# A two-layer decoder trunk: the projection tiles of the double memory step are spread differently over its units

## The chip, the cores and the metric

One core of a Trainium2 chip. The metric is the device time of one execution, in microseconds (us). The engines: TensorE (PE) multiplies matrices, ScalarE (ACT) and VectorE (DVE) do everything elementwise, GpSimd (POOL) helps with copies and sums, SyncE's queue (SP) issues the weight loads. Every engine works through its own program in order; engines wait for each other through semaphores.

## The reference

A trunk of two layers on x of 512 x 1024, with 256 memory tokens, 12 mixing heads and 4 memory heads of 64 columns. Layer A mixes by chunked spatial gating, layer B by forgetting attention (FoX) with keys, values and forget gates from `kv_w`. In each layer the 4 memory heads attend to the memory:

```python
z = x @ b_w_q[j]                      # queries: 12 mixing heads, then 4 memory heads
kvf = x @ kv_w                        # keys, values, forget logits
logcum = cumsum(log_sigmoid(f_logit + kv_b_f))
mix = fox_attention(q, k_sh, v_sh, logcum)
p = softmax(qm . mk * scale);  mo = p . mv          # memory attention
y = concatenate([mix, mo]) @ w_o[layer]
x = layer_norm(DN_ALPHA * x + y);  x = layer_norm(DN_ALPHA * x + sq_relu_mlp(x))
```

## The kernel before

Activations are held transposed, as 8 tiles of 128 features x 512 tokens. Every float32 operand is split in a high and a low part (`x_hi`, `x_lo`, `w_hi`, `w_lo`), and a product is three matmuls: high by high, high by low, low by high. A projection block is 128 output columns: 8 k tiles (one for each 128 rows of the weight), so 24 matmuls of 512 columns into one PSUM bank. Its weight of 128 x 1024 is loaded by SP's queue into one of two places of `w_raw`; ScalarE writes the high part (`prepare`, L1066), VectorE the low one (`prepare`, L1464, which records at L1462) and raises `w_split`. The first k tile of a block waits for that semaphore; a block's last one raises `w_used`.

Layer B's attention is made in steps. A step works on 8 units; a unit is a block of 128 queries. For each unit, in order: PE makes scores (into one of two PSUM banks), VectorE takes the row maximum (`row_max`, L1518 in this step), ScalarE the exponentials (L1125), VectorE normalises them (L1528, L1532), PE transposes the result two units later (`turn`, L561), and ScalarE and VectorE write the high and the low part of the transposes. Behind the units PE does the attention products of each half of the step (`attend`).

The first such step of layer B is the double memory step (`STEP_B`): all 4 memory heads at once, two in each unit, and units 0 to 3 for the first pair of heads, 4 to 7 for the second. `attend_pair` makes each pair's products; that of pair 0 comes behind unit 7, that of pair 1 at the end of the step. Between, `cumulate` sums the forget gates over the tokens. The transposes' parts of pair 0 are called `pm_hi`, `pm_lo`, those of pair 1 `pn_hi`, `pn_lo`.

While PE would wait for the others it is given other work: a step carries the three projection blocks (queries, keys, values; 24 k tiles) that the next step needs. The list `at` in `pair_step` of PE's program says where: place n (`filler(n)`) makes the k tiles at[n] to at[n+1]. Tiles 0 to 7 are the query block, 8 to 15 the key block, 16 to 23 the value block. The order of PE's program within unit u is `filler(u)`, the transposes of unit u-2, the scores of unit u. Behind unit 7 come attention 0, transposes 6, `filler(8)`, transposes 7, `cumulate`, `filler(9)`, attention 1, and the transposes of the values (`turn_values`).

The other engines' programs have fixed places for what belongs to these blocks. ScalarE makes the key block's high part in unit 0, the value block's in unit 4, the next step's first in unit 7. VectorE makes the low parts in units 0 and 4, each directly behind that unit's row maximum, and the next step's first behind the transposes of unit 7; `qs` (queries) is written in units 2 and 3, the first half of the keys in `kc` in unit 6, the second after the units. The order of VectorE's program within a unit is row maximum, that low part, the low part of the transposes of unit u-2, normalising of unit u, `qs` or `kc`.

Behind attention 1 ScalarE and VectorE write its result (`mix_hi`, `mix_lo`), the values and the cumulated gates (`cum`), and two rows of `kc` from these; the scores of the next step wait for them. Five more such steps with keys, one without new blocks, the output projection, the layer norm and the MLP follow.

Of the kernel before, what the change touches and what calls it, by code (L numbers as in the profile page):

```python
# [63 lines left out]
def trunk_kernel(nc, x, mem, a_w_in, a_sgu_ln_g, a_sgu_ln_b, a_w_s, a_b_s, kv_w, kv_b_f, b_w_q,  # L64
# [41 lines left out]
    STEP_A, STEP_B, STEP_FOX, STEP_LAST = 0, 2, 3, 8  # L106
# [12 lines left out]
    with ctx:  # L119
# [261 lines left out]
        def double(s):  # L381

            return s.trip is None and s.base == STEP_B
# [5 lines left out]
        def ahead(s):  # L389

            return s.trip is None and s.base == STEP_LAST
# [117 lines left out]
        def _(pe):  # L509
# [12 lines left out]
            def project(b, g, hi, lo, columns=T, order=range(KT), ready=None, parts=(0, KT),  # L522
                        start=True, stop=True):

                bank = proj[g.slot]
                for n in range(*parts):
                    k = order[n]
                    if n == 0:
                        pe.wait_ge(w_split, b.at(1))
                        if start:  # L530
                            wait(pe, proj_free[g.slot], g.half())
                    if ready:
                        ready(n)
                    last = products(bank[:, 0:columns], block_terms(b, k, hi[:, k], lo[:, k]),
                                    start and n == 0, stop and n == KT - 1)
                if parts[1] == KT:
                    last.then_inc(w_used, 1)
# [85 lines left out]
            def turn(s, u):  # L623

                pe.wait_ge(probs_ready, s.at(u + 1, 8))
                tiles = [probs[:, u % 2, j * P:(j + 1) * P] for j in range(keys(s, u))]
                transposes(tr_index(s, u), tiles[::-1] if fox(s) and u >= TT else tiles)
# [16 lines left out]
            def attend(s, head):  # L644

                if double(s):
                    attend_pair(s, head)
                    return
                pe.wait_ge(tr_free, tr_index(s, head * TT + TT - 1).at(1))
                wait(pe, mix_ready, s.at(head - 1, 2))  # L650
                c = step_kind(s).slot
                if fox(s) and head == 0:
                    pe.wait_ge(vt_ready, step_kind(s).at(1))
                tiles = TT if fox(s) else MT
                for j in range(tiles):
                    seen = slice(j * P if fox(s) else 0, T)
                    if fox(s):
                        vh, vl = v_hi[:, c, j], v_lo[:, c, j]
                    else:
                        vh, vl = mv_hi[:, j, c * P:(c + 1) * P], mv_lo[:, j, c * P:(c + 1) * P]  # L660
                    ph, pl = seen_places(s, head, j)
                    last = products(pv[head][:, seen], [(vh, ph), (vh, pl), (vl, ph)], j == 0, j == tiles - 1)
                last.then_inc(pv_done, 1)

            def turn_values(s, j):

                g = j.times(3, G_FOX + 2)
                pe.wait_ge(proj_free[g.slot], g.half(2))
                if double(s):
                    pe.wait_ge(exp_done, s.at(8, 8))  # L670
                else:
                    pe.wait_ge(mix_ready, s.at(1, 2))
                for t in range(TT):
                    last = pe.transpose(values_bank(s)[:, t * P:(t + 1) * P], v_tmp[:, g.slot, t * P:(t + 1) * P], ident[:, :])
                last.then_inc(vt_done, 1)

            def pair_step(s, b=None, g=None, values=None, extra=None):

                at = [0, 5, 7] if s.base in (STEP_A, STEP_B) else [0, 3, 6]
                at += [8, 11, 14, 16, 18, 19, 21, 24]

                def filler(n):
                    if b is not None:
                        c = at[n] // KT
                        project(b.plus(c), g.plus(c), x_hi, x_lo, parts=(at[n] - c * KT, at[n + 1] - c * KT))
                    elif extra:
                        for part in extra.get(n, ()):  # L690
                            out_start(1, *part)
                for u in range(8):
                    filler(u)
                    if ahead(s):
                        scores(s, u)
                    if u >= 2:
                        turn(s, u - 2)
                    if not ahead(s):
                        scores(s, u)
                attend(s, 0)  # L700
                turn(s, 6)
                filler(8)
                turn(s, 7)
                if s.base == STEP_B:
                    cumulate()
                filler(9)
                attend(s, 1)
                if values is not None:
                    turn_values(s, values)
# [45 lines left out]
            def out_start(layer, c, n):  # L755

                def ready(n):
                    if layer:
                        pe.wait_ge(mix_ready, 2 * STEP_B + n + 1 if n < 2 else 2 * (STEP_FOX + n - 2) + 2)
                    elif n < 2:  # L760
                        pe.wait_ge(mix_ready, 2 * n + 2)
                    else:
                        pe.wait_ge(sgu_ready, 2 * (n - 1))
                project(Pos(B_WO[layer] + c), Pos(G_WO[layer] + c), mix_hi, mix_lo, order=out_order,
                        ready=ready, parts=(n, n + 1))
# [207 lines left out]
            def cumulate():  # L973

                pe.wait_ge(f_act, 3)
                pe.wait_ge(f_step, 5)
                pe.wait_ge(tri_set, 2)
                pe.wait_ge(exp_done, 8 * STEP_B + 7)
                for t in range(TT):
                    span = tri_r[:, 0:T - t * P]  # L980
                    last = products(sc[0][:, t * P:T], [(lf_hi[:, t], span), (lf_lo[:, t], span)],
                                    t == 0, t == TT - 1)
                last.then_inc(cum_done, 1)
# [31 lines left out]
            for s in range(2):  # L1015
                pair_step(Pos(STEP_A + s), Pos(B_AU + 3 * s), Pos(G_AU + 3 * s))
# [23 lines left out]
            turn_forget_gate()  # L1040
            pe.wait_ge(lf_ones, 2)
            pair_step(Pos(STEP_B), Pos(B_FOX), Pos(G_FOX), values=Pos(0))
            with pe.Fori(0, 2) as i:
                for j in range(2):
                    pair_step(Pos(STEP_FOX + j, i, 2), Pos(B_FOX + 3 * (j + 1), i, 6),
                              Pos(G_FOX + 3 * (j + 1), i, 6), values=Pos(j + 1, i, 2))
# [1084 lines left out]
```

## Time and profile before

| | us |
|---|---|
| median of 3 runs | 1207.45 |
| lowest, highest | 1206.73, 1207.56 |
| the profiled execution | 1207.21 |
| its span, first to last instruction | 1205.5 |
| PE, DVE, ACT, POOL busy | 1161.2, 632.7, 491.2, 129.3 |
| mean granted clock of PE | 0.992 |

The profile is one execution. The double step's first projection tile starts 598.31 us after the span's start. Times of instructions are from there too. A matmul's start is a record, its end is modelled; where matmuls follow each other the distance between starts says what one costs. PE's granted clock is 1.00 at 2.4 GHz and 0.50 at 1.2 GHz.

### The profile page before, as it was taken

The page shows a single profiled execution, that of the slowest core. Times are in us where ns is not written, and L with a number is a line of the kernel's source. Part 1 is how long each engine was busy: PE and PEld are TensorE (multiplying, and loading weights), DVE is VectorE, ACT ScalarE, POOL GpSimd, SP SyncE. Part 2 cuts the span into 40 slices and gives each one's busy share as a digit, 9 for nine tenths or more (in the row PEclk, how much of TensorE's full clock was granted, in tenths as well). Part 3 has the DMA queues.
Part 4 walks back from the last instruction along what each step waited for, and adds up shares of the span by engine and source line. Part 5 has one row for each costly group of instructions (what it writes and reads, how often), then busy time and mean ns, then how long its engine had stood idle before and what let it go on. Part 6 is the DMA issues. An engine that isn't in the chain of part 4 may idle for free.

```text
span 1205.5 us, 16763 instructions
## 1 busy us (share of the span) xinstructions
PE 1161.2 (96%) x5888; PEld 976.6 (81%) x5888; DVE 632.7 (52%) x1032; ACT 491.2 (41%) x852; POOL 129.3 (11%) x156
## 2 busy tenths in 40 slices
PE   5998999999999999999998999999999999999997
PEld 5777779888888888789877888878888888888886
DVE  4477766644332445345576777866544323445226
ACT  4445535634211333224665555635543212334120
POOL 2300025100000000023300000026200000000000
PEclk9999999999999999999998999999999999999999
DMA  7422122333323333332311122212333333333332
GB/s 219 134 70 71 53 90 86 88 89 103 105 87 104 88 101 91 105 88 73 86 35 53 54 70 62 60 53 84 93 104 90 102 104 87 88 98 93 105 105 87
DMA packets 185590, 107.22 MB, mean 89 GB/s; under 512 B 4482, under 2 KB 180162, under 8 KB 185540
## 3 DMA queue, kind: packets, MB, share of 16 engines
q1 hardware_dynamic: 180112, 99.36, 28.5%
q10 hardware_dynamic: 5428, 7.18, 1.9%
q8 instruction: 32, 0.52, 0.2%
q14 instruction: 18, 0.15, 0.0%
HBM read 104.43 MB, written 2.10 MB: 88 GB/s over the span
## 4 chain that ended last, share of the span: by engine, by line
PE 74%; DVE 4%; ACT 4%; issue 3%; POOL 1%; DMA 0%; DVEq 0%; ACTq 0%; POOLq 0%; SPq 0%
PE proj L513 59%; PE pv L513 3%; PE sc L513 2%; PE proj L846 2%; PE pv L846 2%; PE tr L846 2%; PE sc L846 2%; PE tr L561 1%; DVE w_lo L1462 1%; ACT w_hi L1066 1%; ACT x L1232 1%; ACT x_hi L1234 1%; POOL total L2054 0%; DVE split_lo L1462 0%; POOL total L2064 0%
## 5 line engine op out<-in xcount | busy, mean ns | idle before, releaser
L1462 DVE TENSOR_TENSOR w_lo<-w_raw,w_hi 128x1024 fp32r<-128x1024 f32 x173 | 219.6, 1270 | 172.3 <-ACT w_hi L1066 124.2
L513 PE MATMUL proj<-x_hi,w_hi 128*128 128x512 f32 (+1 forms) x768 | 300.5, 393 | 1.9 <-ACT relu L1097 1.0
L513 PE MATMUL proj<-x_hi,w_lo 128*128 128x512 f32 (+1 forms) x768 | 295.9, 386 | 0.0
L513 PE MATMUL proj<-x_lo,w_hi 128*128 128x512 f32 (+1 forms) x768 | 289.8, 384 | 0.0
L1066 ACT CAST w_hi<-w_raw 128x1024 fp32r<-128x1024 f32 x160 | 166.9, 1044 | 168.6 <-PE proj L513 166.9
L513 PEld LDWEIGHTS proj<-x_hi,w_hi 128*128 128x128 f32 x768 | 146.1, 190 | 28.9 <-ACT x_hi L1234 2.2
L513 PEld LDWEIGHTS proj<-x_hi,w_lo 128*128 128x128 f32 x768 | 145.8, 190 | 29.2
L513 PEld LDWEIGHTS proj<-x_lo,w_hi 128*128 128x128 f32 x768 | 143.1, 189 | 25.7
L513 PE MATMUL proj<-h_hi,w_hi 128*128 128x512 f32 (+1 forms) x384 | 146.4, 381 | 2.5 <-DVE w_lo L1462 2.5
L513 PE MATMUL proj<-h_lo,w_hi 128*128 128x512 f32 (+1 forms) x384 | 146.0, 380 | 0.0
L513 PE MATMUL proj<-h_hi,w_lo 128*128 128x512 f32 (+1 forms) x384 | 146.0, 380 | 0.0
L1755 DVE TENSOR_TENSOR h_raw<-relu 128x512 f32<-128x512 f32 x64 | 44.3, 692 | 157.7 <-ACT relu L1097 157.7
L1097 ACT ACTIVATE relu<-proj 128x512 f32<-128x512 f32 x64 | 38.2, 597 | 196.0 <-PE proj L513 196.0
L513 PEld LDWEIGHTS proj<-h_hi,w_hi 128*128 128x128 f32 x384 | 72.2, 188 | 16.8 <-DVE w_lo L1462 3.1
L513 PEld LDWEIGHTS proj<-h_lo,w_hi 128*128 128x128 f32 x384 | 72.2, 188 | 13.8
L513 PEld LDWEIGHTS proj<-h_hi,w_lo 128*128 128x128 f32 x384 | 72.2, 188 | 13.7
L1129 ACT ACTIVATE probs<-sc,neg_max 128x128 f32<-128x128 f32 (+2 forms) x64 | 33.0, 516 | 55.9 <-DVE neg_max L1521 54.9
L2005 POOL TENSOR_TENSOR x_lo<-x,x_hi 128x256 fp32r<-128x256 f32 (+1 forms) x56 | 48.5, 875 | 58.0 <-ACT x L1230 24.8
L1462 DVE TENSOR_TENSOR h_lo<-h_raw,h_hi 128x512 f32 (+1 forms) x64 | 44.3, 692 | 14.9 <-ACT h_hi L1246 14.4
L2054 POOL TENSOR_TENSOR total<-x 128x512 f32<-128x512 f32 x3 | 4.5, 1499 | 440.9 <-DVE x L1672 440.9
L513 PE MATMUL proj<-mix_hi,w_hi 128*128 128x256 f32 (+1 forms) x128 | 45.8, 358 | 2.5 <-DVE w_lo L1462 2.2
L1665 DVE SCALAR_TENSOR_TENSOR x<-x,proj 128x512 f32 (+1 forms) x22 | 15.1, 687 | 61.0 <-PE proj L513 61.0
(344 smaller groups left out, 1805.4 us busy)
## 6 DMA issues: line engine op xcount, KB each, us to landing
w_raw<-in_w_up SPq DMA_DIRECT2D x64, 512.0 KB, 4.0
w_raw<-in_w_down SPq DMA_DIRECT2D x64, 512.0 KB, 3.6
w_raw<-in_w_o SPq DMA_DIRECT2D x16, 512.0 KB, 3.6
w_raw<-in_a_w_in SPq DMA_DIRECT2D x14, 512.0 KB, 3.8
w_raw<-in_kv_w SPq DMA_DIRECT2D x12, 512.0 KB, 3.9
w_raw<-in_mem_w_kv SPq DMA_DIRECT2D x8, 512.0 KB, 4.9
w_raw<-in_b_w_q SPq DMA_DIRECT2D x8, 512.0 KB, 3.6
x_nat<-in_x ACTq DMA_DIRECT2D x2, 1024.0 KB, 11.4
```

The costliest lines, as they stand in the source:

```text
L513: last = pe.matmul(target, lhs, rhs, start=start and n == 0, stop=stop and n == len(terms) - 1)
L561: last = pe.transpose(tr[t.slot][0:n, at:at + rows], piece, ident[0:rows, 0:rows])
L846: last = pe.matmul(rows_of[t][n][:, :], lhs, rhs, start=False, stop=stop and m == 2, skip_group_check=True)
L1066: act.copy(weights(b)[0], w_raw[:, b.slot]).then_inc(w_hi_ready, 1)
L1097: act.activation(target, proj[g.slot][:, 0:target.shape[-1]], function).then_inc(proj_free[g.slot], 1)
L1129: act.activation(probs[:, u % 2, 0:n], sc[u % 2][:, 0:n], ACT.Exp, bias=neg_max[:, u:u + 1], accum_out=row_sum[:, u:u + 1]).then_inc(exp_d ...
L1232: act.activation(x32[:, k, own], x32[:, k, own], ACT.Identity, **gain).then_inc(fin_ready, 1)
L1234: act.copy(x_hi[:, k, own], x32[:, k, own]).then_inc(x_hi_ready, 1)
L1462: return dve.tensor_tensor(target, whole, hi.bitcast(F32), ALU.subtract)
L1665: dve.scalar_tensor_tensor(out=tile if target is None else target, in0=tile, scalar=ALPHA if first else 1.0, in1=proj[g.slot][:, :], op0=A ...
L1755: dve.tensor_tensor(raw, wide, wide, ALU.mult).then_inc(relu_sq, 1)
L2005: pool.tensor_tensor(x_lo[:, k, own], x32[:, k, own], x_hi[:, k, own].bitcast(F32), ALU.subtract).then_inc(x_ready, 1)
```

## The change

The list of places for the double step gets its own numbers; the other steps keep theirs (the step in question took the list of `STEP_A` before).

```diff
--- before.py
+++ after.py
@@ -679,8 +679,10 @@
 
 
 
-                at = [0, 5, 7] if s.base in (STEP_A, STEP_B) else [0, 3, 6]
+                at = [0, 5, 7] if s.base == STEP_A else [0, 3, 6]
                 at += [8, 11, 14, 16, 18, 19, 21, 24]
+                if double(s):
+                    at = [0, 6, 8, 11, 13, 16, 18, 20, 21, 22, 24]
 
                 def filler(n):
                     if b is not None:
```

As k tiles of each place, for the double step: 5, 2, 1, 3, 3, 2, 2, 1, 2, 3 before and 6, 2, 3, 2, 3, 2, 2, 1, 1, 2 after. The key block (tile 8) starts at place 2 and not 3, the value block (tile 16) at place 5 and not 6. The programs of the other engines are as before.

## Rows read from the trace of the kernel before

**Rows 1.** The page's busy times: us (share of the span), instructions of each engine.

```profile
PE 1161.2 (96%) x5888; PEld 976.6 (81%) x5888; DVE 632.7 (52%) x1032; ACT 491.2 (41%) x852; POOL 129.3 (11%) x156
```

**Rows 2.** Stretches (us from start): length, busy us (instructions) by engine, granted clock, DMA.

```profile
core 0: us, PE busy (x) PEld busy (x) DVE busy (x) ACT busy (x) POOL busy (x), PEclk, DMA share, GB/s
598.30:634.25 35.95, 33.25 (x170) 27.16 (x169) 25.53 (x58) 24.39 (x60) 2.65 (x4) 0.95 0.13 36
634.25:640.45 6.20, 2.69 (x14) 1.97 (x13) 4.42 (x7) 3.18 (x5) 0.00 (x0) 0.90 0.23 70
661.60:688.00 26.40, 26.40 (x145) 22.49 (x144) 20.36 (x44) 15.23 (x36) 2.44 (x4) 1.00 0.22 61
```

**Rows 3.** PE in order of time: start, us, engine, line, operation, [idle before <- releaser].

```profile
598.31 0.50 PE L513 MATMUL proj<-x_hi,w_hi 128*128 128x512 f32 x1
...
601.86 0.28 PE L513 MATMUL sc<-mk_rest,qm 128*128 128x256 f32 x1
...
602.33 0.40 PE L513 MATMUL proj<-x_hi,w_hi 128*128 128x512 f32 x1
...
607.04 0.66 PE L561 MATMUL tr<-ident,probs 128*128 128x128 f32 x4 [1.98 <-DVE probs L1532]
...
609.27 0.63 PE L513 MATMUL proj<-x_lo,w_hi 128*128 128x512 f32 x1
609.70 0.63 PE L513 MATMUL proj<-x_hi,w_lo 128*128 128x512 f32 x1
...
612.45 0.28 PE L513 MATMUL sc<-mk_twice,qm 128*128 128x256 f32 x1
...
617.72 0.28 PE L513 MATMUL sc<-mk_twice,qm 128*128 128x256 f32 x1
618.13 0.50 PE L513 MATMUL proj<-x_hi,w_hi 128*128 128x512 f32 x1
...
619.61 0.60 PE L561 MATMUL tr<-ident,probs 128*128 128x128 f32 x4
...
620.40 0.28 PE L513 MATMUL sc<-mk_twice,qm 128*128 128x256 f32 x1
620.52 0.40 PE L513 MATMUL proj<-x_hi,w_hi 128*128 128x512 f32 x1
...
629.41 0.45 PE L513 MATMUL proj<-x_hi,w_hi 128*128 128x512 f32 x1
...
631.53 0.39 PE L513 MATMUL pv<-pn_hi,mv_hi 128*128 128x512 f32 x1
...
640.45 0.44 PE L513 MATMUL sc<-kc,qc 128*128 128x128 f32 x1 [3.51 <-DVE kc L1614]
```

**Rows 4.** VectorE in order of time, same columns.

```profile
604.07 1.22 DVE L1462 TENSOR_TENSOR w_lo<-w_raw,w_hi 128x1024 fp32r<-128x1024 f32 x1
...
609.40 0.69 DVE L1518 TENSOR_REDUCE neg_max<-sc 128x2 f32<-128x512 f32 x1
...
612.02 0.68 DVE L1596 SCALAR_TENSOR_TENSOR qs<-proj,qs 64x512 fp32r<-64x512 f32 x1
612.77 0.69 DVE L1518 TENSOR_REDUCE neg_max<-sc 128x2 f32<-128x512 f32 x1
...
616.13 0.69 DVE L1518 TENSOR_REDUCE neg_max<-sc 128x2 f32<-128x512 f32 x1
616.85 1.23 DVE L1462 TENSOR_TENSOR w_lo<-w_raw,w_hi 128x1024 fp32r<-128x1024 f32 x1
...
619.32 0.68 DVE L1518 TENSOR_REDUCE neg_max<-sc 128x2 f32<-128x512 f32 x1
...
621.82 0.68 DVE L1518 TENSOR_REDUCE neg_max<-sc 128x2 f32<-128x512 f32 x1
...
630.50 0.69 DVE L1462 TENSOR_TENSOR pn_lo<-tr,pn_hi 128x512 fp32r<-128x512 f32 x1
```

**Rows 5.** Stretches again, at the lower granted clock.

```profile
608.60:611.90 3.30, 3.30 (x11) 2.52 (x10) 2.67 (x8) 2.27 (x8) 0.15 (x1) 0.50 0.01 2
640.50:646.00 5.50, 5.50 (x16) 4.63 (x17) 1.83 (x5) 0.46 (x2) 0.00 (x0) 0.50 0.33 95
```

## The prediction

> **What bounds the kernel now.** First the page's busy times: TensorE works for 1161.2 of 1205.5 us, VectorE for 632.7, ScalarE for 491.2 [rows 1]. So time is saved or lost where PE stands still or runs at its lower clock. The busy time by stretch shows where that is: a key/query step further on is PE from end to end (26.40 of 26.40 us, granted clock 1.00), while the double step is not (33.25 of 35.95 us at 0.95), and in the 6.20 us behind it PE works 2.69 [rows 2]. The instructions in order of time give the places: the first transposes wait 1.98 us for `probs`, and the next step's first scores 3.51 for `kc` [rows 3]; unit 5's transposes show a short wait of the first kind.
>
> The question is whether the waits for `probs` are PE's to lose. They are not. VectorE goes round: row maximum of unit u, (ScalarE's exponentials), reciprocal, normalising, row maximum of unit u+1. The maxima of units 2 to 6 start at 609.40, 612.77, 616.13, 619.32 and 621.82 [rows 4]. The scores for them lay ready: the last score matmul of unit 5 was issued at 617.72 and ended at 618.00, 1.3 us ahead of its maximum [rows 3, 4]. Only unit 3 is near PE: its last one ends at 612.45 + 0.28 = 612.73, the maximum starts at 612.77, but `qs` holds VectorE to 612.02 + 0.68 = 612.70 anyway [rows 3, 4]. So the step's pace is that of VectorE and ScalarE, and PE's fillers lie in their shade; what reaches the end is the moment at which head pair 1's attention starts (631.53). Everything up to the next step's scores hangs on that one after another (PE, `mix_hi`, `mix_lo`, `v_lo`, `cum`, `kc`), and the steps behind it are all PE [rows 2, 3]. A shift of 631.53 is a shift of the end.
>
> **The change part by part.** No instruction is added or removed; 24 k tiles (72 matmuls) stay between the same scores and transposes, in another place. They cost PE the same, and only the waits that they meet change. Prices for PE at full clock: five tiles take 601.86 − 598.31 = 3.55 (0.71 each, two 1.42), three take 631.53 − 629.41 = 2.12; a first unit's scores take 602.33 − 601.86 = 0.47, transposes with the next scores 620.52 − 619.61 = 0.91 [rows 3].
>
> Unit 0, six tiles: scores 0 start at 598.31 + 3.55 + 0.71 = 602.57 and end about 603.2. Their maximum (0.69 long) ended as `w_lo` began, at 604.07 [rows 4], so it started about 603.4 and doesn't move. Unit 1, two tiles, then scores 1: PE is free at 602.57 + 0.47 + 1.42 + 0.47 = 604.93.
>
> Unit 2 now opens the second block (keys), so it needs that block's `w_lo`, which VectorE writes from 604.07 to 605.29 [rows 4]. PE waits 0.4 us, and runs three tiles from 605.34 to 607.46. The transposes of unit 0 start then and not at 607.04; with scores 2 they are done at 608.37. Maximum 2 only starts at 609.40 [rows 4], so this too costs nothing, and most of the 1.98 us idle is filled.
>
> Unit 3, two tiles: 609.79; transposes 1 and scores 3 end at 610.70 (before 612.73). Maximum 3 can then start straight behind `qs`, some 0.1 us earlier; I take a gain of 0.1 (0 to 0.15) for all that follows on VectorE. Unit 4, three tiles: 612.82; transposes 2 and scores 4: 613.73.
>
> Unit 5 is the place that matters. Its two tiles are now tiles 16 and 17, the first of the third block (values). They wait for that block's split, and VectorE's program has it in unit 4, behind maximum 4: it runs 616.85 to 618.08, directly behind that maximum [rows 4]; ScalarE's half isn't the limit. Before, these tiles stood in unit 6 and met the wait with PE only some 0.3 us early (restart at 618.13). Now PE gets there at 613.73 and stands for 4.4 us. Queued behind the waiting matmul are transposes 3 and scores 5, which were long done before (ended 618.00). VectorE can't run maximum 5 until they come, and its lo half of transposes 3, normalising 5 and maximum 6 are queued behind it.
>
> The length comes from an identical row of before: from the same split, PE ran two tiles, transposes and scores, 618.13 to 620.40 + 0.28 = 620.68 [rows 3]. So maximum 5 starts at 620.72 and not at 619.32: +1.4 us. Then the clock. After 1.98 us idle, PE worked a while and was then granted 0.50 (its lower level, 1.2 GHz) from 608.6 to 611.9 though busy; after 3.51 us idle it has 0.50 through 640.5 to 646.0; the step without idle has 1.00 [rows 2, 3, 5]. Now 4.4 us idle stand right before the two tiles, so I expect that they, the transposes and the scores run low. A 512-column matmul is then issued every 0.43 us (609.27 to 609.70) and not every 0.23 (a third of 0.71) [rows 3]. All low: six matmuls 6 × 0.20 = 1.2, and of the 0.91 for transposes and scores nearly as much again, estimated at 0.7: 1.9 us. All high: 0. The low stretch may begin or end inside these 4 us, so I take 1.6, and keep 0 and 1.9 as ends. The Trainium skill ("TensorE: Matmul & The Clock Gate", Back-to-back issue gap) gives N/1.2 ns low and N/2.4 + 2.5 high, 427 and 216 ns for 512 columns; the rows agree for low and have some 235 for high. By the page six matmuls would lose 1.27 us.
>
> So maximum 5 moves by 1.4 + 1.6 − 0.1 = +2.9. From there to the end of the step the old row applies, if PE keeps up: two tiles, transposes 4 and scores 6 take 1.42 + 0.91 behind scores 5 at full clock, 2.3 us, and maximum 6 comes 621.82 − 619.32 = 2.50 behind maximum 5 [rows 4]. It keeps up with 0.2 to spare; were the clock still low then, up to 0.5 more would be lost. Units 7, 8 and 9 have one, one and two tiles in place of one, two and three.
>
> At the end the cover shrinks and shows a small gain. Transposes 7 wait for normalising 7 as before. Behind them come the cumulation, three tiles from 629.41, and attention 1 at 631.53 [rows 3]; with two tiles PE would be ready 0.7 earlier, at 630.82. VectorE's `pn_lo` for unit 7 ends at 630.50 + 0.69 = 631.19 [rows 4], so attention 1 starts at about 631.25: −0.28 against 631.53. The block's end comes earlier too, but `v_tmp` is wanted only behind attention 1.
>
> Sum: 1.4 + 1.6 − 0.1 − 0.3 = +2.6 us. The profiled execution took 1207.21 us (its span 1205.5), so 1209.8; it lies 0.24 under the median of the three runs, 1207.45. On that median: 1210.05, said as 1210.1. One thing remains that I can't place: the low stretch behind the next step's idle (640.45 to 646.0 at half speed: 5.5 / 2 = 2.8 us lost) depends on where the idle falls. I take no change, and keep 1.3 less and 0.5 more as its ends.
>
> **Rivals.** A, the clock doesn't fall in those 4 us: only the wait remains, 1.4 − 0.1 − 0.3 = +1.0, 1208.4. For it, nothing in the rows; against it, two shorter idles were followed by low stretches.
>
> B, the wait is harmless because work queued behind it on PE passes it: maximum 5 stays at 619.2, and only the two small gains are left, −0.4, 1207.1. Against it: in the profile scores 2 too ran only behind transposes 0, which waited.
>
> C, other side, faster: the double step is PE's to win after all. Place: the 1.98 us wait of unit 0 and the low stretch 608.6 to 611.9 that follows it. Both go with the three tiles moved there, 1.98 − 0.4 + 3.3/2 = 3.2 us, 1204.2. It decides if VectorE's maxima 1 to 4 follow PE and the values split comes before 613.7; the rows have them following VectorE.
>
> D, the low clock lasts so long that scores 6 and the transposes behind them are late also: +1.9 for the clock, +0.5 for unit 6, +0.5 in the next step: about +4, 1211.5.
>
> **Chances.** Forecast (wait and low clock) 0.72; A 0.12; B 0.05; C 0.04; D 0.07. A difference under 0.2% (2.4 us here) is about what a measurement of this kernel can't tell from no change. The forecast lies at 2.6 with 1.9 to 3.2 around it: somewhat over half of it is beyond 2.4, 0.41, with D 0.48. C makes faster 0.04; the rest, 0.48, is within. The range: from between B and A (1207.9) to D's lower half (1211.4).
>
> **What would show it.** PE waits for `w_lo` at the first matmul of unit 5, some 4.4 us, from 613.7 to 618.0; the wait for `probs` 0 is gone; the maximum of unit 5 starts at about 622.2 and that of unit 4 at 616.0; the granted clock is low somewhere in 618 to 622.5; attention 1 starts at about 634.1 and directly behind `pn_lo`. I am wrong if maximum 5 starts before 620.5, if the low clock isn't there, or if the 2.6 us don't appear unchanged at the next step's `kc`.

## The result and the profile after

Over 22 executions of each, the changed kernel has a median of 1208.99 us and the kernel before 1207.23; the ratio is 1.0022, with a 95% interval of 1.0014 to 1.003, so +2.7 us (1.7 to 3.6). The forecast was +2.6, on the median of 1207.45 known then 1210.1. The ratio isn't the quotient of the two medians: these lie 1.8 us apart, at the low end of the interval, and the measured median of 1208.99 is 1.1 under the forecast one. One of the changed kernel's 22 executions took 6564.85 us and is left out of the ratio; nothing on record says why it did.

The profiled execution took 1213.15 us (span 1211.4), far above that median. 3.68 us of its surplus over the span of before lie ahead of the double step, whose first tile starts at 601.99 and not 598.31. There its clock was low where that of before was up (1.00 from 190 to 200); half speed for 6 us loses 3.0 of them:

```profile
193.50:199.50 6.00, 6.00 (x30) 6.00 (x30) 0.80 (x5) 0.29 (x1) 0.00 (x0) 0.50 0.00 0
```

That is this execution, not the change: the second profile of experiment 7 below, which is built on the kernel before, has the same low stretch there and its first tile at 601.90. So everything here is compared from the step's first tile on. A unit's row maximum is called "maximum" with the unit's number, and "length" is the time from the step's first tile to attention 1.

The stretches (length, busy us by engine, granted clock) are, for the kernel before, the step to attention 1; for the changed kernel, the same, the part from there to the next step's first scores, and the low stretch within the step.

```profile
598.31:631.53 33.22, 30.52 (x159) 24.95 (x157) 24.03 (x57) 23.78 (x59) 2.65 (x4) 0.95 0.13 36
601.99:638.35 36.36, 31.08 (x158) 25.61 (x157) 23.81 (x57) 24.09 (x60) 2.65 (x4) 0.91 0.11 32
638.35:647.40 9.05, 5.54 (x26) 4.29 (x26) 6.19 (x9) 3.59 (x6) 0.00 (x0) 0.97 0.23 58
619.80:626.10 6.30, 4.35 (x14) 3.67 (x15) 3.15 (x6) 1.55 (x5) 0.00 (x0) 0.50 0.32 86
```

The step's length to attention 1 is 36.36 and was 33.22 (598.31 to 631.53, [rows 3]): +3.14. The next part is 9.05 and was 8.92 (to 640.45): +3.27 together. Up to attention 1 PE is busy for 31.08 us and was for 30.52; it stands for 5.28 (36.36 − 31.08) and stood for 2.70. Its clock is 0.91 and was 0.95.

PE of the changed kernel in order of time; they answer to [rows 3].

```profile
601.99 0.50 PE L513 MATMUL proj<-x_hi,w_hi 128*128 128x512 f32 x1
...
609.02 0.50 PE L513 MATMUL proj<-x_hi,w_hi 128*128 128x512 f32 x1 [0.30 <-DVE w_lo L1464]
...
611.20 0.60 PE L561 MATMUL tr<-ident,probs 128*128 128x128 f32 x4
...
617.27 0.28 PE L513 MATMUL sc<-mk_twice,qm 128*128 128x256 f32 x1
621.75 0.79 PE L513 MATMUL proj<-x_hi,w_hi 128*128 128x512 f32 x1 [4.20 <-DVE w_lo L1464]
622.34 0.63 PE L513 MATMUL proj<-x_lo,w_hi 128*128 128x512 f32 x1
622.77 0.63 PE L513 MATMUL proj<-x_hi,w_lo 128*128 128x512 f32 x1
...
624.48 1.05 PE L561 MATMUL tr<-ident,probs 128*128 128x128 f32 x4
...
625.97 0.41 PE L513 MATMUL sc<-mk_twice,qm 128*128 128x256 f32 x1
626.18 0.52 PE L513 MATMUL proj<-x_hi,w_hi 128*128 128x512 f32 x1
...
638.35 0.50 PE L513 MATMUL pv<-pn_hi,mv_hi 128*128 128x512 f32 x1 [0.23 <-DVE pn_lo L1464]
638.69 0.40 PE L513 MATMUL pv<-pn_lo,mv_hi 128*128 128x512 f32 x1
...
647.40 0.45 PE L513 MATMUL sc<-kc,qc 128*128 128x128 f32 x1 [3.51 <-DVE kc L1616]
```

The 1.98 us for `probs` is gone (transposes 0 start at 611.20 without a wait; 0.30 us for the keys' `w_lo` stands ahead of them). In its place stand 4.20 us for `w_lo`: scores 4 end at 617.27 + 0.28 = 617.55, and the value block's first tile starts at 621.75. Then the tiles run at the lower clock (622.34 to 622.77 is 0.43), transposes 3 start at 624.48, and scores 5 end at 625.97 + 0.41 = 626.38. At the end attention 1 starts 0.23 us late by PE's reckoning, for `pn_lo`.

VectorE of the changed kernel, against [rows 4]; the last row is a split in the next step.

```profile
619.75 0.69 DVE L1520 TENSOR_REDUCE neg_max<-sc 128x2 f32<-128x512 f32 x1
620.47 1.22 DVE L1464 TENSOR_TENSOR w_lo<-w_raw,w_hi 128x1024 fp32r<-128x1024 f32 x1
...
626.42 0.69 DVE L1520 TENSOR_REDUCE neg_max<-sc 128x2 f32<-128x512 f32 x1 [3.40 <-PE sc L513]
...
628.93 0.68 DVE L1520 TENSOR_REDUCE neg_max<-sc 128x2 f32<-128x512 f32 x1
...
637.60 0.69 DVE L1464 TENSOR_TENSOR pn_lo<-tr,pn_hi 128x512 fp32r<-128x512 f32 x1
...
661.49 1.22 DVE L1464 TENSOR_TENSOR w_lo<-w_raw,w_hi 128x1024 fp32r<-128x1024 f32 x1
```

Maximum 4 is at 619.75 − 601.99 = 17.76 us behind the first tile (before 17.82), the split directly behind it. Maximum 5 is at 24.43; before 21.01: +3.42. Maximum 6 is 2.51 behind it (before 2.50), `pn_lo` ends at 638.29, and attention 1 starts 0.06 behind that. The last row, the first split behind the next low stretch, comes 59.50 us behind the first tile. Before it came 55.91 behind it:

```profile
654.22 1.23 DVE L1462 TENSOR_TENSOR w_lo<-w_raw,w_hi 128x1024 fp32r<-128x1024 f32 x1
```

So there the shift is +3.59.

### The profile page after: what moved, and what is told of

It reads as the page before. It is cut to its first block, busy times and chain, and to the rows that moved or that the text cites. A ratio compares the mean times of both kernels' runs of the same rounds, so it can differ in the third digit from the quotient of the medians.

```text
span 1211.4 us, 16763 instructions
## 1 busy us (share of the span) xinstructions
PE 1164.2 (96%) x5888; PEld 979.6 (81%) x5888; DVE 632.6 (52%) x1032; ACT 491.3 (41%) x852; POOL 129.3 (11%) x156
## 4 chain that ended last, share of the span: by engine, by line
PE 73%; ACT 5%; DVE 5%; issue 3%; POOL 1%; DMA 0%; DVEq 0%; ACTq 0%; POOLq 0%; SPq 0%
PE proj L513 59%; PE pv L513 3%; PE sc L513 2%; PE proj L848 2%; PE sc L848 2%; PE pv L848 2%; PE tr L848 2%; PE tr L561 1%; DVE w_lo L1464 1%; ACT w_hi L1068 1%; ACT x L1234 1%; ACT x_hi L1236 1%; ACT probs L1127 1%; POOL total L2056 0%; PE sc L815 0%
```

## The experiments

All places in the step are given in us behind its first tile, which is the first row of each fence; waits and lengths are durations. The code is cut to the lines edited. Time ratios are to the kernel before, measured on the same chip. The fences of this section show all engines in order of time; only the rows read are given.

**1. Value block back at place 6** (on the changed kernel)

```diff
-                    at = [0, 6, 8, 11, 13, 16, 18, 20, 21, 22, 24]
+                    at = [0, 6, 8, 11, 13, 16, 16, 18, 20, 22, 24]
```

> The changed kernel's first five places (6, 2, 3, 2, 3), but the value block starts at place 6 again and place 5 is empty: 6, 2, 3, 2, 3, 0, 2, 2, 2, 2. From the step's first projection tile to attention 1 the kernel before took 33.2 us, the changed one 36.4. Theory (transposes 3 and scores 5 queued behind the wait for the values' split cost it): maximum 5 comes 20.9 to 21.0 us after the step's first tile as before (changed kernel 24.4). PE now stands about 3.5 us before place 6, with a low clock behind it, so scores 6 may be 0 to 1 late: length 33.0 to 34.5, time +0 to +1.2 on the kernel before. Rival, the front (key block opened at place 2, transposes 0 later) costs it: length 36 as in the changed kernel, and maxima 1 to 4 late.

```profile
598.00 0.50 PE L513 MATMUL proj<-x_hi,w_hi 128*128 128x512 f32 x1
...
617.78 0.55 PE L513 MATMUL proj<-x_hi,w_hi 128*128 128x512 f32 x1 [1.57 <-DVE w_lo L1464]
...
618.96 0.68 DVE L1520 TENSOR_REDUCE neg_max<-sc 128x2 f32<-128x512 f32 x1
...
621.96 0.69 DVE L1520 TENSOR_REDUCE neg_max<-sc 128x2 f32<-128x512 f32 x1 [0.40 <-PE sc L513]
...
631.74 0.39 PE L513 MATMUL pv<-pn_hi,mv_hi 128*128 128x512 f32 x1
```

Measured: ratio 0.9999 (0.9985 to 1.0012). Maximum 5 is back at 20.96, with the changed front in place, so the front is harmless and the rival falls. PE stands in two pieces, 1.50 us for `probs` ahead of transposes 3 and 1.57 for `w_lo` ahead of place 6, not 3.5 in one. The granted clock is 0.50 from 618.5 to 621.0 behind the second, and scores 6 are 0.40 us late; the length is 33.74, +0.5.

**2. PE kept busy ahead of place 5** (on the changed kernel)

```diff
                 for u in range(8):
+                    if u == 5 and double(s):
+                        for _ in range(17):
+                            products(pv[0][:, :], [(x_hi[:, 0, 0:P], x_hi[:, 0])])
                     filler(u)
```

> The changed kernel with 17 matmuls of 512 columns more, into the idle bank of attention 0, ahead of place 5 (their product isn't used, the output is the same). They fill some 3.9 of the 4.2 us that PE stands there; the wait for the split ends when it did, and the two tiles, transposes 3 and scores 5 stay behind it. Theory (1.4 us of wait and 1.2 to 1.9 of low clock): the clock stays at its upper level, maximum 5 comes 22.3 us after the step's first tile (before 21.0, changed kernel 24.4), length to attention 1 34.3, time about +1.0 on the kernel before. Rival, the wait alone makes the loss and the clock would have been lost anyway: maximum 5 at 24 as in the changed kernel, +2.6.

```profile
598.62 0.50 PE L513 MATMUL proj<-x_hi,w_hi 128*128 128x512 f32 x1
...
618.38 0.50 PE L513 MATMUL proj<-x_hi,w_hi 128*128 128x512 f32 x1 [0.32 <-DVE w_lo L1467]
...
621.01 0.69 DVE L1523 TENSOR_REDUCE neg_max<-sc 128x2 f32<-128x512 f32 x1 [1.36 <-PE sc L513]
...
632.95 0.50 PE L513 MATMUL pv<-pn_hi,mv_hi 128*128 128x512 f32 x1 [0.24 <-DVE pn_lo L1467]
```

Measured: 1.0013 (1.0002 to 1.0024), +1.6 us (0.2 to 2.9). Maximum 5 is at 22.39: the wait ends when it did and two tiles, transposes and scores stand behind it, but at the upper clock. The wait alone is 22.39 − 21.01 = 1.38, the clock 24.43 − 22.39 = 2.04 in the first profile. This split rests on the places in the profiles: in time, the intervals of this kernel and of the changed one overlap.

**3. The split made in unit 3** (on the changed kernel; ScalarE's `prepare` in units 0, 3, 7, VectorE's in 0, 3, of which the latter is shown)

```diff
-                    if reading and u in (0, 4):
-                        prepare(b.plus(u // 4 + 1))
+                    places = (0, 3) if double(s) else (0, 4)
+                    if reading and u in places:
+                        prepare(b.plus(places.index(u) + 1))
```

> The changed kernel, with ScalarE's and VectorE's halves of the value block's weight made in unit 3 and not 4 of the double step. Theory: the split is ready 14.8 us or so after... the step's first tile plus 16.4 (changed kernel: 19.7), and PE's wait for it goes from 4.2 to some 1 us; but the value block's bank is only free when VectorE has written qs in unit 3, which now stands 1.2 us later, at about 18.5 after the first tile, so PE still stands some 3 us, now for qs. Maximum 5 then at 21.2 (clock high) to 23.1 (low), length 33 to 35, time +0 to +2. Rival, the split isn't what the tiles wait for: maximum 5 stays at 24.4 and time at +2.6.

```profile
598.49 0.50 PE L513 MATMUL proj<-x_hi,w_hi 128*128 128x512 f32 x1
...
616.95 0.47 PE L513 MATMUL proj<-x_hi,w_hi 128*128 128x512 f32 x1 [2.93 <-DVE qs L1599]
...
619.53 0.69 DVE L1521 TENSOR_REDUCE neg_max<-sc 128x2 f32<-128x512 f32 x1
...
631.48 0.50 PE L513 MATMUL pv<-pn_hi,mv_hi 128*128 128x512 f32 x1 [0.23 <-DVE pn_lo L1465]
```

The wait became one of 2.93 us for `qs`, as expected: the value block takes the PSUM bank of the query block, which `qs` frees. Maximum 5 is at 21.04 and the length 32.99, shorter than before. But the timing is 1.0023 (1.001 to 1.0036), +2.8 us, above the expected 0 to 2. The profiled execution had its clock up behind this wait and was the shortest of twelve (1205.97, median 1208.67). So it was profiled again.

> The same kernel as e3_split_early, for a second profile: its first had the clock up behind the wait for qs of 2.9 us (maximum 5 at 21.0 us behind the step's first tile, length 33.0), though its median was 2.8 us above the kernel before. Theory: the clock does fall behind that wait in other executions; if it does in this one, maximum 5 comes at 22 to 23 and the length is 34 to 35. If length is 33.0 again, the median isn't explained by it.

Measured: 1205.93 us, wait 2.92, maximum 5 at 21.00, length 32.95, no low clock in the step: a miss. The median isn't explained by these profiles. The mean granted clock that each execution has on record says what kind of time it is: six of the twelve have 0.988 or 0.989 and took 1209.5 to 1212.4 us, while the two profiled ones have 0.995 and none of 35 executions of the kernel before has under 0.990. Over the twelve the mean is 0.9904, over the 35 it is 0.9925, which by itself is 0.0021 of 1207, 2.5 us. So the surplus is about what the lower clock makes; that it falls behind this wait is possible and not shown.

**4. One tile at place 5** (on the changed kernel)

```diff
-                    at = [0, 6, 8, 11, 13, 16, 18, 20, 21, 22, 24]
+                    at = [0, 6, 8, 11, 13, 16, 17, 19, 21, 22, 24]
```

> As the changed kernel, but one tile at place 5, the rest later: 6, 2, 3, 2, 3, 1, 2, 2, 1, 2. Theory (what is queued between the end of the wait and scores 5 counts tile by tile): maximum 5 comes one tile earlier than in the changed kernel, 0.7 us at the upper and 1.3 at the lower clock: 23.1 to 23.7 after the step's first tile; length 35.1 to 35.7, time +1.3 to +2.0 on the kernel before. Rival, the late places cost it (one tile, not two, behind transposes 6): with those unchanged but for one tile, the length stays at 36.4 and the time at +2.6.

```profile
599.01 0.50 PE L513 MATMUL proj<-x_hi,w_hi 128*128 128x512 f32 x1
...
622.17 0.69 DVE L1520 TENSOR_REDUCE neg_max<-sc 128x2 f32<-128x512 f32 x1 [2.12 <-PE sc L513]
...
625.47 0.69 DVE L1520 TENSOR_REDUCE neg_max<-sc 128x2 f32<-128x512 f32 x1 [0.71 <-PE sc L513]
...
635.12 0.51 PE L513 MATMUL pv<-pn_hi,mv_hi 128*128 128x512 f32 x1 [0.38 <-DVE pn_lo L1464]
```

Its granted clock over the tiles, transposes and scores behind the wait:

```profile
617.50:624.00 6.50, 5.23 (x16) 4.41 (x17) 3.85 (x8) 2.71 (x10) 0.00 (x0) 0.50 0.32 83
```

Measured: 1.0017 (1.0003 to 1.0031), +2.1 us. Maximum 5 is at 23.16, 1.27 us earlier than in the changed kernel's first profile: one tile at the lower clock (3 × 0.43). But the length is 36.11, above the 35.1 to 35.7 expected. Most of the gain was given back one unit later: maximum 6 waits 0.71 us for scores 6 and is 3.30 behind maximum 5 and not 2.50, since two tiles, transposes 4 and scores 6 partly ran low. A tile taken away from behind the wait has to be made in a later unit, and there it cost nearly as much.

**5. Only the late places** (on the kernel before: 5, 2, 1, 3, 3, 2, 2, 2, 2, 2; two tiles at place 9 as in the changed kernel, where places 7 and 8 have one each)

```diff
                 at += [8, 11, 14, 16, 18, 19, 21, 24]
+                if double(s):
+                    at = [0, 5, 7, 8, 11, 14, 16, 18, 20, 22, 24]
```

> The kernel before with one tile moved from place 9 to place 7: 5, 2, 1, 3, 3, 2, 2, 2, 2, 2. This is the late part of the change alone, without the wait at unit 5. Theory: the low part of transposes 7 then sets attention 1, and not PE's third tile: length from the step's first tile to attention 1 32.9 to 33.0 (before 33.22), time -0.3 on the kernel before, below what the clock's variation lets be timed. Rival, fewer tiles behind transposes 7 leave PE without cover and cost time: length 33.5 or more and a time of +0.5 or more.

```profile
598.79 0.50 PE L513 MATMUL proj<-x_hi,w_hi 128*128 128x512 f32 x1
...
618.58 0.50 PE L513 MATMUL proj<-x_hi,w_hi 128*128 128x512 f32 x1 [1.57 <-DVE w_lo L1464]
...
631.69 0.50 PE L513 MATMUL pv<-pn_hi,mv_hi 128*128 128x512 f32 x1 [0.24 <-DVE pn_lo L1464]
```

Measured: length 32.90, with 0.24 us of PE waiting for `pn_lo`: −0.32 against 33.22. In time 1.0004 (0.9992 to 1.0016), which can't show so little. The next step's scores come 41.97 behind the first tile (before 42.14): half of the gain is gone again, as attention 1 now starts from a standstill (its first matmul takes 0.34 to the next, 638.35 to 638.69 in the changed kernel, and took 0.22 before).

This profile shows one thing more. It has the front places of the kernel before, but no low clock behind the first transposes' wait (2.02 us here). PE is done with scores 5 at 18.21 and not at 19.69, and stands for the difference: 1.57 us for `w_lo`. So the low stretch at 608.6 to 611.9 of the kernel before cost nothing.

**6. PE kept busy ahead of `kc`** (on the kernel before)

```diff
                 if values is not None:
                     turn_values(s, values)
+                if double(s):
+                    for _ in range(14):
+                        products(tr[0][:, :], [(x_hi[:, 0, 0:P], x_hi[:, 0])])
```

> The kernel before with 14 matmuls of 512 columns more (into a free transposes bank, the product isn't used, the output is the same) behind the transposes of the values, where PE stands 3.51 us for kc. Theory (an idle of this length is followed by a low clock whose price lies on the path to the end): the idle shrinks to about 0.3, the clock stays at its upper level into the next step, time -1.2 to -2.8 on the kernel before, 1204.1 to 1205.7. Rival, low clock here is hidden or comes anyway: 0.

```profile
600.00 0.50 PE L513 MATMUL proj<-x_hi,w_hi 128*128 128x512 f32 x1
...
642.16 0.30 PE L513 MATMUL sc<-kc,qc 128*128 128x128 f32 x1 [0.34 <-DVE kc L1617]
```

Measured: 0.9989 (0.9977 to 1.0001), −1.3 us (−2.8 to +0.1). The wait for `kc` is 0.34 and the clock is up behind it; the scores come when they did (42.16). The interval just reaches no change. The profile is clearer: the split that came at 55.91 comes at 53.35, 2.56 earlier.

**7. Both of the last two together**, twice; the rows are of the second profile

> Both edits of the last two on the kernel before: spread 5, 2, 1, 3, 3, 2, 2, 2, 2, 2, and 14 unused matmuls ahead of the wait for kc. The sum of the two: length to attention 1 33.0, no low clock behind it, time -1.5 to -3.1, 1203.8 to 1205.4 if the kernel before takes 1206.9. If the low clock is hidden there: -0.3.

> The same kernel as h_tail_busy, to halve the interval of its time: the first measurement was 0.9991 (0.9981 to 1.0002) of the kernel before. Theory 0.998 to 0.9995; if the low clock is hidden there 0.9998 to 1.0002.

```profile
601.90 0.50 PE L513 MATMUL proj<-x_hi,w_hi 128*128 128x512 f32 x1
...
643.85 0.30 PE L513 MATMUL sc<-kc,qc 128*128 128x128 f32 x1 [0.34 <-DVE kc L1619]
```

Measured: 0.9991 (0.9981 to 1.0002), then 0.9982 (0.9968 to 0.9996): −1.1 and −2.2 us, of which the first is less than the 1.5 expected at least. Medians 1205.35 and 1205.14 against 1206.8 and 1206.2. The lengths are 32.93 and 32.89, and no low clock stands behind `kc` in either. The second interval is clear of no change and the first just reaches it. Against the changed kernel (1.0014 to 1.003) both are clear; against the kernel before the gain is small and rests on the second.

**8. The changed kernel, second profile**

> The changed kernel again, for a second profile, since the place at which PE's clock falls differs between executions. Theory: the wait for w_lo at unit 5 is 4.2 us again; maximum 5 comes 22.3 us behind the step's first tile if the clock stays up and up to 24.4 if it is low all the way, most likely 23.5 to 24.4. Rival (the clock's part of the first profile was an exception): 22.3 to 22.6.

```profile
598.59 0.50 PE L513 MATMUL proj<-x_hi,w_hi 128*128 128x512 f32 x1
...
618.39 0.73 PE L513 MATMUL proj<-x_hi,w_hi 128*128 128x512 f32 x1 [4.24 <-DVE w_lo L1464]
...
622.59 0.69 DVE L1520 TENSOR_REDUCE neg_max<-sc 128x2 f32<-128x512 f32 x1 [2.92 <-PE sc L513]
...
634.54 0.50 PE L513 MATMUL pv<-pn_hi,mv_hi 128*128 128x512 f32 x1 [0.23 <-DVE pn_lo L1464]
```

Measured: 1209.28 us; wait 4.24, maximum 5 at 24.00, length 35.95, next scores at 45.00 (before 42.14: +2.86), the split in the next step at 58.74 (+2.83). The low clock costs 24.00 − 22.39 = 1.61 here and 2.04 in the first profile.

**9. The changed kernel with PE busy in both idles** (the edits of experiments 2 and 6 together)

> The changed kernel with unused matmuls in both of its long idles: 17 ahead of place 5 and 14 ahead of the wait for kc. What is left of the change is the wait at unit 5 (+1.1 us in length) without a low clock, and the kernel before's low clock ahead of the next step is gone too. Theory: length from the step's first tile to attention 1 34.3, no low clock from there to 50 us behind that tile, time +1.1 - 1.4 = about -0.3 on the kernel before, and about 2 under e2's +1.6. Rival, the low clock ahead of the next step costs nothing: as e2_keep_busy, +1.0 to +1.6.

```profile
599.46 0.50 PE L513 MATMUL proj<-x_hi,w_hi 128*128 128x512 f32 x1
...
619.25 0.50 PE L513 MATMUL proj<-x_hi,w_hi 128*128 128x512 f32 x1 [0.35 <-DVE w_lo L1470]
...
621.85 0.69 DVE L1526 TENSOR_REDUCE neg_max<-sc 128x2 f32<-128x512 f32 x1 [1.34 <-PE sc L513]
...
633.78 0.50 PE L513 MATMUL pv<-pn_hi,mv_hi 128*128 128x512 f32 x1 [0.23 <-DVE pn_lo L1470]
...
642.85 0.30 PE L513 MATMUL sc<-kc,qc 128*128 128x128 f32 x1 [0.33 <-DVE kc L1622]
```

The whole step and 7 us of the next one:

```profile
599.46:650.00 50.54, 48.68 (x251) 39.82 (x250) 34.32 (x77) 30.55 (x74) 2.96 (x5) 1.00 0.16 45
```

Measured: 1.0001 (0.9987 to 1.0014), +0.1 us where −0.3 was expected. Maximum 5 is at 22.39 again, the length 34.32, and there is no low clock. Against experiment 2 the ratio is 0.0012 lower, 1.4 us, the expected price of the low clock behind `kc`; but the two intervals overlap, and the two were measured on different chips.

## Why the prediction held, step by step

**What bounds the step.** Maxima 0 to 4 come 5.16, 8.60, 11.10, 14.41 and 17.76 us behind the first tile in the changed kernel; those of units 2 to 4 came at 11.09, 14.46 and 17.82 before [rows 4]. PE's fillers lay in VectorE's shade, and rival C (3.2 us to win there) fell with it. Experiment 5 says the same from the other side, where the low stretch that C counted is absent and nothing is won. For the gain of 0.1, 0.06 stands in the profile (17.82 to 17.76), but the reason given for it was wrong: experiments 5 and 7 have the front places of the kernel before and maximum 4 at 17.78 and 17.77 in the two profiles without that low stretch. What is won there is the stretch's absence, not the tiles' new places.

**The wait at unit 5.** PE reached the tile at 617.55, 15.6 us behind the first, and stood 4.20 us (4.4 forecast). The row of before that stood for the length, 618.13 to 620.68, was the right one: experiment 2 shows 1.38 for wait and queue without the clock. Experiment 1 moves the wait to place 6, behind scores 5, and the loss goes. Rival B (work queued behind the waiting matmul passes it) fell: scores 5 came behind the two tiles in every profile that has the wait at place 5.

**The clock.** Forecast 1.6, ends 0 and 1.9. Measured 2.04 and 1.61 by the difference of two profiles of the changed kernel and the one with PE kept busy (22.39 in two kernels). The upper end was 0.14 too low. The rows of the first profile give the whole: the start 621.75 to 622.34 is 0.59 against 0.34, five more matmuls lose 0.20 each, and transposes and scores take 624.48 to 626.18, 1.70 against 0.91, a loss of 0.79 where 0.7 had been estimated: 0.25 + 1.0 + 0.79 = 2.04. Rival A (clock up) didn't occur in either profile of the changed kernel. That the clock is part of the loss in the other executions too is supported by the mean granted clock: 0.9911 over the 21 of the changed kernel, 0.9921 to 0.9925 in the three sets of the kernel before that stand beside the experiments, which is 1.2 to 1.7 us of 1208.

**The margin of 0.2 us at unit 6.** It held in both profiles of the changed kernel (maximum 6 is 2.51 behind maximum 5). Experiments 1 and 4 show it used up, by 0.40 and 0.71 us of waiting, so rival D was near. That it held is partly luck: it depends on where the low stretch ends, which the prediction couldn't say.

**The end of the step.** −0.28 by `pn_lo`; measured 3.42 − 3.14 = 0.28, and −0.32 alone in experiment 5. What I had not seen is that PE restarts from a standstill there: 0.13 us are lost again before `kc` (9.05 against 8.92).

**The sum.** To the next step's scores +3.27 and +2.86 in two profiles, +2.7 (1.7 to 3.6) timed. The forecast of 2.6 is lower than both profiles by its clock price, which is that of the second and 0.4 under that of the first, and by the 0.13 of the restart. The mechanism is shown; that 2.6 and 2.7 lie so close is luck, as the interval is nearly 2 us wide and the medians give 1.8. Nor do the profiles keep their shift to the end. It is +3.59 and +2.83 at the split in the next step, and +2.2 and +1.8 at the end of the spans (1211.4 − 601.99 and 1207.6 − 598.59 against 1205.5 − 598.31), since the profile of the kernel before has one more low stretch (0.54 from 799.5 to 803.2) that these two lack. The shift of 631.53 goes on into the next step, as the prediction said; low stretches elsewhere come on top and differ between executions. The chances lay level between "within 0.2%" and "slower by more"; the ratio 1.0022, with an interval on both sides of 1.002, leaves that as open as it was.

**What I couldn't place**, the low stretch ahead of the next step, stayed: it ends about 47.8 us behind the first tile before, 51.7 and 50.6 in the two profiles of the changed kernel, 4.0 and 2.9 later, so it moved with the scores and took 0.3 us more in the first profile. Experiments 6, 7 and 9 give its price in time: 1.1 to 2.2 us (with some 0.2 for the late places in 7). That is under the 2.8 that half speed over 5.5 us makes, and that experiment 6 won back in its profile (2.56 at the split), because it isn't that long in every execution: 3.4 us in experiment 2, 6.8 in experiment 3. In experiment 2 the split comes at 654.73 − 598.62 = 56.11, only 0.20 later than before though the scores were 1.25 late; a shorter stretch can hide a shift in a single profile.

Open is where the executions of experiment 3 lose their 2.8 us, which the two profiles, both of short executions, don't show.

## What to carry to other kernels

A filler between two engines' turns is free only while everything that it waits for is there: before moving one to fill an idle, look up which program makes its operand and what is queued behind it. Here the operand came from the very engine whose pace the filler was to follow, so the block could not start earlier, and the wait held up two instructions that were ready. An idle of PE can also have a second price behind it, in the clock: for its upper end count the work that stands directly behind the wait at half speed, and if the idle can't be filled with useful work, unused matmuls can be worth their place.

## What the runs showed of the hardware

Idles of about 4.2 us ahead of place 5 were followed by a low clock in all three profiles that have them (both of the changed kernel, and experiment 4), one of 2.9 us in neither of two (experiment 3), while an idle of 1.98 to 2.02 us ahead of the first transposes was followed by one in the profiles of before, of experiment 6 and of the first of experiment 7, and not in those of experiment 5 and of the second of experiment 7. In experiment 1 two idles of 1.50 and 1.57 us, 1.1 us apart, had a low clock behind them. All profiles with the 3.51 us idle ahead of `kc` have a low stretch behind it. Length of idle alone doesn't tell. Filling an idle down to 0.3 us kept the clock at its upper level behind it each time (experiments 2, 6, 7 and 9). The Trainium skill ("TensorE: Matmul & The Clock Gate", What's actually happening) has the lower level as the default that activity releases. These runs agree: 14 and 17 matmuls without a use kept it away. Executions of one kernel differ by up to 5 us (before 1204.61 to 1209.71) with their low stretches in different places: the first profile of the changed kernel was 3.68 us late before it reached the changed code.
